# A two-layer trunk on one core: the up projections of its MLPs with weights as the stationary operand, in products of 256 columns

## The reference, cut to what matters

```python
def squared_relu_mlp(h, w_up, w_down):
    return jnp.square(jax.nn.relu(h @ w_up)) @ w_down

h = h + rms_norm(mixer(rms_norm(h, g[0])), g[1])
h = h + rms_norm(squared_relu_mlp(rms_norm(h, g[2]), w_up, w_down), g[3])
```

## Time and profile before

| | |
|---|---|
| median of 3 runs | 1970.49 us (1968.65 to 1971.59) |
| the profiled execution | 1969.32 us, its span 1967.5 us |
| instructions in the trace | 26643 |
| PE busy | 1949.2 us, 8914 products |
| PEld busy | 1604.4 us, 8914 loads |
| DVE busy | 1076.0 us |
| ACT busy | 972.3 us |
| HBM read | 365.51 MB, 187 GB/s over the span |

### The profile page before, as it was taken

How to read it: one execution, slowest core, us unless ns; L and a number is a source line. 1 busy time by engine, 2 the same in 40 slices (tenths; PEclk the granted TensorE clock), 3 DMA queues, 4 the chain that set the end, 5 groups by cost and what they waited for, 6 DMA issues and landing times.

```text
span 1967.5 us, 26643 instructions
## 1 busy us (share of the span) xinstructions
PE 1949.2 (99%) x8914; PEld 1604.4 (82%) x8914; DVE 1076.0 (55%) x1276; ACT 972.3 (49%) x1339; POOL 6.2 (0%) x23
## 2 busy tenths in 40 slices
PE   7999999999999999999999999999999999999998
PEld 6777888888888888888888888888888888888886
DVE  6676574554454445445667655654544544544454
ACT  6665475435534543554554444654345335434542
POOL 0000000000000000000000000000000000000000
PEclk9999999999999999999999999999999999999999
DMA  6545566565555555555475655565555565555553
GB/s 234 173 139 176 198 205 200 183 199 181 186 192 189 178 199 194 179 186 198 142 256 174 196 184 186 172 210 199 194 173 190 194 194 189 181 198 188 182 191 107
DMA packets 189833, 368.40 MB, mean 187 GB/s; under 512 B 12616, under 2 KB 12752, under 8 KB 189008
## 3 DMA queue, kind: packets, MB, share of 16 engines
q1 hardware_dynamic: 187264, 360.75, 55.7%
q0 software_dynamic: 1040, 6.82, 1.0%
q10 hardware_dynamic: 1472, 0.08, 0.0%
HBM read 365.51 MB, written 2.10 MB: 187 GB/s over the span
## 4 chain that ended last, share of the span: by engine, by line
PE 97%; DMA 1%; DVE 1%; ACT 1%; issue 0%; SPq 0%; DVEq 0%; ACTq 0%
PE acc L357 31%; PE acc L359 31%; PE acc L358 31%; PE t L378 2%; DMA w_raw<-in_attn_w_qkv 1%; PE t L391 0%; PE scores L459 0%; PE o L481 0%; PE t L469 0%; PE scores L591 0%; ACT a_hi L650 0%; DVE w_lo L983 0%; DVE a_lo L1004 0%; PE t L439 0%; ACT b_hi L679 0%
## 5 line engine op out<-in xcount | busy, mean ns | idle before, releaser
L983 DVE TENSOR_TENSOR w_lo<-w_raw,w_hi 128x1024 fp32r<-128x1024 f32 x680 | 820.4, 1223 | 629.0 <-ACT w_hi L630 600.1
L630 ACT ACTIVATE w_hi<-w_raw 128x1024 fp32r<-128x1024 f32 x680 | 708.2, 1058 | 620.1 <-PE acc L359 588.7
L357 PE MATMUL acc<-w_hi,a_hi 128*128 128x512 f32 x1440 | 573.6, 398 | 3.2 <-DVE a_lo L1004 2.9
L359 PE MATMUL acc<-w_hi,a_lo 128*128 128x512 f32 x1440 | 563.2, 391 | 0.0
L358 PE MATMUL acc<-w_lo,a_hi 128*128 128x512 f32 x1440 | 562.3, 390 | 0.0
L357 PE MATMUL acc<-w_hi,b_hi 128*128 128x512 f32 x1280 | 500.9, 391 | 0.0
L359 PE MATMUL acc<-w_hi,b_lo 128*128 128x512 f32 x1280 | 498.4, 389 | 0.0
L358 PE MATMUL acc<-w_lo,b_hi 128*128 128x512 f32 x1280 | 498.2, 389 | 0.0
L357 PEld LDWEIGHTS acc<-w_hi,a_hi 128*128 128x128 f32 x1440 | 271.4, 188 | 60.9 <-DVE a_lo L1004 4.2
L359 PEld LDWEIGHTS acc<-w_hi,a_lo 128*128 128x128 f32 x1440 | 271.1, 188 | 58.1
L358 PEld LDWEIGHTS acc<-w_lo,a_hi 128*128 128x128 f32 x1440 | 271.6, 189 | 53.7
(11 more groups left out here) (120 smaller groups left out, 476.0 us busy)
## 6 DMA issues: line engine op xcount, KB each, us to landing
w_raw<-in_mlp_w_up SPq DMA_DIRECT2D x256, 512.0 KB, 4.1
w_raw<-in_mlp_w_down SPq DMA_DIRECT2D x256, 512.0 KB, 4.4
w_raw<-in_sgu_w_in SPq DMA_DIRECT2D x64, 512.0 KB, 4.5
w_raw<-in_attn_w_qkv SPq DMA_DIRECT2D x40, 512.0 KB, 4.8
w_raw<-in_attn_w_o SPq DMA_DIRECT2D x32, 512.0 KB, 4.2
w_raw<-in_sgu_w_out SPq DMA_DIRECT2D x32, 512.0 KB, 4.3
gain<-in_norm_gains POOLq DMA_DIRECT2D x4, 1024.0 KB, 6.0
h<-in_x SPq DMA_DIRECT2D x8, 256.0 KB, 6.5
```

What stands on the lines that cost most here:

```text
L357: nc.tensor.matmul(acc[t][:, :], lhsT=x_hi[:, kb, tok], rhs=w1, start=(kb == 0), stop=False)
L359: last = nc.tensor.matmul(acc[t][:, :], lhsT=x_lo[:, kb, tok], rhs=w1, start=False, stop=(kb == KB - 1))
L630: nc.scalar.activation(w_hi[:, i % SLOTS, :], w_raw[:, i % RAW_SLOTS, :], ACT.Copy).then_inc(hi_made, 1)
L983: nc.vector.tensor_tensor(w_lo[:, i % SLOTS, :], w_raw[:, i % RAW_SLOTS, :], w_hi[:, i % SLOTS, :].bitcast(F32), ALU.subtract).then_inc(lo ...
```

## The change

In 15 of the 16 up blocks of each MLP the operands change places. A 128x128 piece of w_hi or w_lo is stationary, and the 256 tokens of a_hi or a_lo are the moving operand. The output of a block lies in four banks (f = 0 to 3), 128 hidden columns on partitions and 256 tokens on columns in each, so a down block can use it without a transpose. Successive up blocks alternate between the banks t, acc and scores, o. DVE reads two banks at a time with ReLU and the scale in one instruction, ACT squares twice (once rounded to b_hi, once plain into s), and DVE subtracts to b_lo.

Since tokens are now on columns, r_in is needed along the columns on all partitions. DVE multiplies the unit matrix by r_in, TensorE multiplies that by a matrix of ones (`spread_r`), and DVE copies the result to r_all, once for each layer. The first up block of each MLP is as before. a_hi and a_lo become two halves of one buffer; the first down block of a quarter may start before the last up block is read out; the four up blocks of a quarter are written out rather than looped over.

```diff
+            def up_block(q, blk, j):
+                banks = [pair[:, f, :] for pair in up_banks[j % 2] for f in range(2)]
+                for i in range(2 * PAIRS):
+                    pe.wait_ge(lo_made, blk * (2 * PAIRS) + (i + 1))
+                    for f in range(4):
+                        if i == 0 and f == 0:
+                            pe.wait_ge(acc_free, blk * 2 - 2)
+                        if i == 0 and f >= 2 and j == 0:
+                            pe.wait_ge(acc_free, blk * 2 + (f - 3))
+                        for k in range(SLAB_KB):
+                            kb = i * SLAB_KB + k
+                            col = slice(k * COL + f * P, k * COL + (f + 1) * P)
+                            for c in range(2):
+                                nc.tensor.matmul(banks[f][:, 0:SEQ], lhsT=w_hi[:, i % SLOTS, col],
+                                                 rhs=a[:, kb, c, :], start=(kb == 0 and c == 0), stop=False)
+                            last = nc.tensor.matmul(banks[f][:, 0:SEQ], lhsT=w_lo[:, i % SLOTS, col],
+                                                    rhs=a[:, kb, 0, :], start=False, stop=(kb == KB - 1))
+                        if i == 2 * PAIRS - 1 and f == 1:
+                            last.then_inc(half_done, 1)
+                    last.then_inc(slab_used, 1)
+                    if isinstance(q, int) and q == 0 and j == 1:
+                        if i < TOK:
+                            first_to_b(i)
+                        elif i == TOK:
+                            spread_r(blk)
...
-                def down(q, blk, j, hooks):
+                def first_down(q, blk):
                     for pair in range(PAIRS):
-                        if hooks and pair == PAIRS - 1:
-                            pe.wait_ge(t_lo, q * (8 * NB) + 4 * (use0 + UNITS + 2 * NB))
+                        pe.wait_ge(b_ready, 2 * w_index(layer, q, pair + 1))
                         for half in range(TOK):
-                            multiply(blk, b_hi, b_lo, pair, half)
-                            for step in (hooks or {}).get((pair, half), ()):
-                                step()
+                            multiply(blk, b_hi, b_lo, pair, half, early=True)
...
+                def square_to_b(q, blk, j):
+                    for p in range(2):
+                        act.wait_ge(acc_free, 2 * blk + p + 1)
+                        nc.scalar.activation(b_hi[:, 4 * j + 2 * p:4 * j + 2 * p + 2, :], up_tiles(p), ACT.Square)
+                        nc.scalar.activation(up_tiles(p), up_tiles(p), ACT.Square).then_inc(b_hi_made, 1)
...
+                def rectify(blk, j):
+                    r = r_all[:, :].unsqueeze(1).to_broadcast([P, 2, SEQ])
+                    for p in range(2):
+                        product_done(dve, blk, p)
+                        nc.vector.scalar_tensor_tensor(out=up_tiles(p), in0=up_banks[j % 2][p][:, :, 0:SEQ], scalar=0.0,
+                                                       in1=r, op0=ALU.max, op1=ALU.mult).then_inc(acc_free, 1)
+                def low_of_b(q, j):
+                    for p in range(2):
+                        dve.wait_ge(b_hi_made, 2 * w_index(layer, q, j) + p + 1)
+                        at = (slice(None), slice(4 * j + 2 * p, 4 * j + 2 * p + 2))
+                        nc.vector.tensor_tensor(b_lo[at], up_tiles(p), b_hi[at].bitcast(F32), ALU.subtract
+                                                ).then_inc(b_ready, 1)
...
+                        if first and j == 1:
+                            for t in range(TOK):
+                                split_s(t, use0 + UNITS + t, 0)
+                            split_ahead(blk + j, 1)
+                            dve.wait_ge(r_filled, layer + 1)
+                            nc.vector.tensor_copy(r_all[:, :], acc[0][:, 0:SEQ]).then_inc(r_spread, 1)
+                            dve.wait_ge(r_spread, layer + 1)
...
+            pool.wait_ge(small_filled, 1)
+            nc.gpsimd.memset(ones[:, :], 1.0).then_inc(consts_made, 1)
+            pool.wait_ge(consts_made, 3 + HALF)
```

More of the change, by code:

```diff
@@ L103, in trunk @@
         y = sb("y", [P, TOK, D])
[L104 to L105 removed]
+        a = sb("a", [P, KB, 2, SEQ], F32R)
         b_hi = sb("b_hi", [P, KB, SEQ], F32R)
@@ L134, in trunk @@
         rot = sb("rot", [P, 4, TOK, GROUP, HALF])
+        rot_flat = rot[:, :, :, :, :].rearrange("p i t h n -> p (i t h n)")
+        r_diag = rot_flat[:, 0:SEQ].rearrange("p (t n) -> p t n", t=TOK)
+        r_all = rot_flat[:, SEQ:2 * SEQ]
+        ones = gain_rows
         sink_rows = sb("sink_rows", [P, KVH * 2, 2])
@@ L146, in trunk @@
         moments = sb("moments", [P, TOK, 2])
+        a_hi, a_lo = a[:, :, 0, :], a[:, :, 1, :]
         yf = y[:, :, :].rearrange("p t n -> p (t n)")
@@ L164, in trunk @@
         wsT = work[:, D:D + SG * P].rearrange("p (g n) -> p g n", g=SG)
[L167 to L172, removed]
+        accs, ts, scores, os = (ctx.enter_context(nc.psum_tensor(name, [P, 2, COL], F32))
+                                for name in ("acc", "t", "scores", "o"))
+        acc, tb, sc, ob = ([banks[:, 0, :], banks[:, 1, :]] for banks in (accs, ts, scores, os))
+        up_banks = [(ts, accs), (scores, os)]
         junk = ob[1]
@@ L242, in product_done, with up_tiles, w_index @@
                 eng.wait_ge(slab_used, (blk + 1) * (2 * PAIRS))
+        def up_tiles(p):
+            return s[:, p, :].rearrange("p (f n) -> p f n", f=2)
+        def w_index(layer, q, j):
+            return q * NB + (W_BLOCKS * layer + j - 1)
         def keys(c):
@@ L364, in multiply_slab, with multiply @@
                     last.then_inc(half_done, 1)
-            def multiply(blk, x_hi, x_lo, pair, t, between=None):
-                multiply_slab(blk, x_hi, x_lo, 2 * pair, t)
+            def multiply(blk, x_hi, x_lo, pair, t, between=None, early=False):
+                multiply_slab(blk, x_hi, x_lo, 2 * pair, t, early=early)
                 if between:
@@ L505, in mlp, with first_to_b @@
             def mlp(base, layer, use0, then):
[L506 to L512, removed]
+                def first_to_b(t):
+                    transpose_s(t, use0 + UNITS + t, squared, layer * TOK + t + 1)
@@ new lines, in spread_r @@
+                def spread_r(blk):
+                    pe.wait_ge(consts_made, 3 + HALF)
+                    pe.wait_ge(r_diag_made, layer + 1)
+                    pe.wait_ge(acc_free, blk * 2)
+                    nc.tensor.matmul(acc[0][:, 0:SEQ], lhsT=ones[:, :],
+                                     rhs=rot_flat[:, 0:SEQ], start=True, stop=True
+                                     ).then_inc(r_filled, 1)
+                def up_block(q, blk, j):
[23 more added lines that the diff above has]
+                                spread_r(blk)
@@ L1071, in first_block @@
                 inverse(r_in)
+                if spread:
+                    dve.wait_ge(norm_done, norms[0])
+                    for t in range(TOK):
+                        last = nc.vector.tensor_scalar(r_diag[:, t, :], ident[:, :], r_in[:, t:t + 1], None, ALU.mult)
+                    last.then_inc(r_diag_made, 1)
                 if layer0:
@@ L1154, in quarter @@
-                    with dve.Fori(1, NB) as j:
-                        split_ahead(blk + j, 0)
-                        up_splits(q, j - 1)
-                        for pair in range(1, PAIRS):
+                        first_block(blk, use0, 4 * layer + 2, spread=True)
+                    for j in range(1 if first else 0, NB):
+                        split_ahead(blk + j, 0)
+                        if first and j == 1:
+                            for t in range(TOK):
+                                split_s(t, use0 + UNITS + t, 0)
+                            split_ahead(blk + j, 1)
+                            dve.wait_ge(r_filled, layer + 1)
+                            nc.vector.tensor_copy(r_all[:, :], acc[0][:, 0:SEQ]).then_inc(r_spread, 1)
+                            dve.wait_ge(r_spread, layer + 1)
+                            rest = (2, 3)
+                        else:
+                            if j > 0:
+                                low_of_b(q, j - 1)
+                            rest = (1, 2, 3)
+                        for pair in rest:
```

55 lines of the change are left out of this document (23 added, 32 removed).

## The result

The changed kernel took 1983.76 us (median of 4 runs, 1982.25 to 1989.63) beside 1969.99 for the kernel before (4 runs): 1.0074 times as long, 95% interval 1.0062 to 1.0087. A second set of 5 runs on another occasion gave 1985.13 us and 1.0078 (1.0064 to 1.0092). So the change costs 14 to 16 us where the forecast was a gain of 22. The value lay within the range and on the wrong side of no change; the second case's number, 1981, was nearly right.

A forecast was written before the change was run, and what follows sets the result against it. TensorE's instruction pitch was taken to bound the kernel: 1969.3 - 29.0 (transposes) + 5.6 (narrow products) + 0.9 (spread) = 1946.8, plus 1.2 for the median, 1948 us; range 1930 to 1993.

The forecast's parts named there:

- the second case: Narrow products: extra paid per product, p = 120.0 ns, recorded duration 0.283, 1981 us in all; chance 0.27.
- What bounds the kernel: Whole kernel: TensorE, busy 99% of the span, so only the pitch of its instructions counts.
- what the change removes: Transposes of s in 30 of 32 up blocks: 0.97 us a block, 29.0 us, all on TensorE's path.
- The spread: r_in's spread, once a layer: one f32 product of 256 columns and a late next start, 0.9 us on TensorE.
- the read-out: Up blocks' banks: ACT and DVE work, with splits 11.0 and 12.7 of 21.9 us; neither becomes the bound.
- the hand-overs: Three places where TensorE might wait: acc's banks, alternating up-block banks, b for the first down block; all at nothing.
- The pitch p of a product of 256 columns: Changed up blocks: start to start with its load, taken as 114.3 ns; 192 a block, +5.6 us for 30 blocks.
- the two readings by columns: Narrow products' pitch if half the extra stays: 114.7 ns, or 113.3 by plain halving.
- the extra: Float32r products at 2.4 GHz: pitch beyond the columns' streaming time, 13.3 ns at 512 columns (226.7 against 213.3).
- the load's 110: Weight loads: each holds its place for 0.110 us, so p cannot be below that.
- The first case: Narrow products: extra goes with the columns, p 113 to 116 ns, 1942 to 1958 us in all; chance 0.46.
- the third case: Narrow products: load and product don't overlap fully, p = 0.126 us or more, 2015 us in all; chance 0.11.

The follow-up runs named there:

- e3: Kernel before with one transpose in place of four for each of the MLPs' 64 hidden-layer tiles; 1947.79 us beside 1969.39, 0.989 times.
- e5: Changed kernel plus series of 512, 384 and 256 columns behind 128, 96, 64 and 32 stationary columns; at 256, pitch 120.0 ns behind 128, 113.3 behind 64.
- e1: Changed kernel plus 16 series of 96 float32r products of 512 to 64 columns, stationary 128 or 64; 256 columns behind 128: 120.0 ns, load floor 111.7.
- e6: Changed kernel run once more, unaltered, on the same chip as other experiments; 1985.13 us (5 runs), 1.0078 times the kernel before.
- e4: Changed kernel with TensorE's loop over the two middle quarters written out; 1981.28 us (5 runs), 1.0058 times the kernel before.
- e7: Changed kernel with w_hi multiplied by a_hi and a_lo in one product of 512 columns, halves added later by DVE; 1966.90 us, 0.9989 times the kernel before.
- e2: Kernel before with 30 up blocks' products cut in two of 256 columns, except first and last row groups; 2003.55 us, 1.0171 times the kernel before.
- e10: e7 with each slab's 8 products of 512 columns by w_hi first, then 8 of 256 by w_lo; 1959.81 us, 0.9951 times the kernel before.
- e9: Changed kernel plus series: 224 to 448 columns behind 64 stationary ones, then 512 and 256 alternating in runs of 1 to 16; alternating means 173.6 to 175.2 ns.

## Why the prediction was wrong, point by point

**What bounds the kernel, and what the change removes:** right. TensorE alone counts. 29.0 us for the transposes stands on e3's measured 0.1125 for each, 27 for 240, and 2 more for the products behind them, which no run measured by themselves.

**The spread, the read-out, the hand-overs:** right. The spread took 0.43 us in each layer (its first instruction starts at 289.10, the second product behind it at 289.65, of which 0.12 is that of a product), 0.9 for both. The reads by DVE took 0.69 (0.75 was reckoned) and the squares 0.62. No wait names them, and the one row that does name DVE was not about it.

**The pitch p of a product of 256 columns: the step that failed.** "I take 114.3, between the two readings by columns." It is 120.0, so 192 p is 23.04 and not 21.95, +38.4 us for +5.6 on the sum: 33 us, all of the error but the branch. The part of the reasoning that looked bold holds in the main: the extra grows with the columns, from 6.7 ns at 128 to 16.7 at 512 behind loads of 64, though unevenly, and its 113.3 for 256 columns is right with some luck. The part that looked safe failed: that the load's 110 is a floor, that the product's time is another, and that p is the larger of the two. Measured, 111.7 for the load and 113.3 for the product (beside a load of 64) give 120.0 together. The first case fails with it. (Its lower end, 1942, belongs to p = 113.3; 113 gives 1940.5.)

What the first bound was read from holds elsewhere in the trace. A load starts with the product before it, and its own product follows 0.23 us later; behind the idle stretch of the earlier trace rows the kernel before goes on with:

```profile
69.19 0.39 PE L358 MATMUL acc<-w_lo,a_hi 128*128 128x512 f32 x1
69.19 0.19 PEld L359 LDWEIGHTS acc<-w_hi,a_lo 128*128 128x128 f32 x1
69.42 0.40 PE L359 MATMUL acc<-w_hi,a_lo 128*128 128x512 f32 x1
```

The product at 68.85, which starts together with its own load, is recorded with 0.50 for 0.39, and the next one comes 0.34 after it for 0.227: 0.11 more both times. The product at 36.77 has the same 0.50, and 0.34 to the next (37.11). Plain float32 at the gates is 216 x 2.4 / 256 = 2.03 clocks a column by its pitch; float32r at 256 columns is 120 x 2.4 / 256 = 1.13.

**The second case** had the number (1981) with a mechanism that e5 refutes: the extra is not paid per product, since a stationary operand of 64 columns takes half of it away at 256 columns. As a price it holds wherever a load of 128 stands before the product, 11.7 to 16.0 ns from 240 to 512 columns. Its sign, a recorded 0.283, could not tell it from the third case: behind loads of 64 the same products are recorded with 0.276. **The third** came nearest with its mechanism, "load and stream are now equally long with no slack", and gave it 126 at least, a price that no row carried. The issue of twice the instructions was not the limit: in e1, products of 64 columns with 64 stationary ones come every 58.3 ns. What was measured is a third case at the second's price, as far as e5 can tell load from output width.

The sum with the measured terms: 1970.0 - 29.0 + 38.4 + 0.9 + 3.9 for the two branches = 1984.2, for 1983.8 measured. That they agree so closely is luck: the second set of runs has 16.0 us between the kernels for the sum's 14.2, and the sum leaves out the start. TensorE's first recorded branch, with 383 products before it in every trace, stands at 90.1 us before, at 94.3 after, at 93.5 in e6 and 93.4 in e4, but at 89.7 in e1 and e7, so the start varies from one profile to the next and no run shows what the change does to it. The cleaner check begins there: to the end of the span the kernel before takes 1877.4 us and e4, which has no long branch, 1887.9. That is 10.5 more, and the sum without the branches has 10.3.

**The granted clock** was to stay at 1.0 in up blocks, or the account would be wrong as a whole. It fell to 0.50 for 3.4 us of one, behind the branch's idle stretch, and stayed at 1.0 there in e6. So the account lacked the branch; it was not wrong as a whole.

**The long branch** was missed altogether. The change's text had it: four up blocks written out in a loop that TensorE goes through twice, 960 products in its body for 384 before.

## What to carry to other kernels

Where two pipelined steps of one engine come out about equally long, as a weight load and a product of 256 columns do here, don't take the larger of the two as the pitch: price the pair by a series of such pairs, or leave a range that holds more than the larger. More and narrower products cost what the narrow width adds to each (84 more a block made e2 34 us slower), so an exchange of operands that removes transposes pays here only with wide products in it, and how two widths are mixed was worth half as much as the whole exchange cost (7 us from e7 to e10). And when an idle stretch at a loop's end is put down to another engine, write the loop out once before believing it.

## What the runs showed of the hardware that was not expected

- A float32r product of 256 columns has a pitch of 113.3 ns behind loads of 64 or 32 stationary columns, 116.0 behind 96 and 120.0 behind 128, though loads of 128 alone need only 111.7. At 384 columns a narrower load gives nothing back, and at 512 the pitch rises from 226.7 to 230.0 and 231.7.
- The pitch of equal products is not steady at first: in e9, after another width, it takes some five products of up to 236 ns to settle at 226.7, and some series (448 columns in e1: 199 to 207 ns; 512 with 64 stationary columns in e5: 224 to 236) did not settle in 96.
- The branch back of a TensorE loop whose body has 960 products took 4.7 to 5.5 us, and the body's instructions came in again; with 704 products (e7) or 384 (before) it took 0.2 and they did not. In the first profile one of the two stretches was followed by 3.4 us at a granted clock of 0.50.
